# A fused two-block kernel: late modulation chunks inside the heads, routing on the unnormalised sum, the norm's gain applied to the gathered features

## The reference

```python
# first block
mix = hybrid_mixer(x, ...)                       # ends in merged @ w_out
h = layer_norm(ALPHA * x + mix, ln1_g, ln1_b)
logits = h @ router_w + router_b                 # 32 experts, the top 4 of each token
gates = softmax(top_4(logits))
ffn = sum over the chosen experts of gate * (act(h @ w_up[e] + b_up[e]) @ w_down[e] + b_down[e])
h = layer_norm(ALPHA * h + ffn, ln2_g, ln2_b)
# second block
mod = silu(c) @ w_ada + b_ada                    # sh1, sc1, g1, sh2, sc2, g2
h1 = ada_norm(x, norm1_g, sh1, sc1)
mixed = concat(neighbourhood(4 heads), latent(8 heads), conv)
mixed = rms_norm over groups of 64 (mixed) * out_norm_g
x = x + g1 * (mixed @ w_out_2)
x = x + g2 * ((silu(gt) * up) @ w_down_2)        # gt, up from ada_norm(x, norm2_g, sh2, sc2) @ w_gu
```

## Time and profile before

| | |
|---|---|
| runs | 1519.65, 1520.72, 1525.38 us |
| the profiled execution | 1522.91 us, span 1521.2 us from the first to the last instruction |
| TensorE matmul busy | 1421.0 us (93%) |
| VectorE, ScalarE, GpSimd busy | 585.2, 446.5, 39.4 us (38, 29, 3%) |
| read from memory | 514.75 MB, 339 GB/s over the span |
| mean granted clock of TensorE | 0.997 of full |

### The profile page before, as it was taken

How to read it: one execution, slowest core, us unless ns; L and a number is a source line. 1 busy time by engine, 2 the same in 40 slices (tenths; PEclk the granted TensorE clock), 3 DMA queues, 4 the chain that set the end, 5 groups by cost and what they waited for, 6 DMA issues and landing times. The chain is left out here.

```text
span 1521.2 us, 19879 instructions
## 1 busy us (share of the span) xinstructions
PE 1421.0 (93%) x8029; PEld 843.9 (55%) x8029; DVE 585.2 (38%) x979; ACT 446.5 (29%) x589; POOL 39.4 (3%) x81
## 2 busy tenths in 40 slices
PE   9999999999999999988988988989889999899998
PEld 9987897344434433333323433423334788788887
DVE  4984556210210221120210210210212685777765
ACT  5654533121112112112111111111102546454343
POOL 2000030000000000000000000000000022000000
PEclk9999999999999999999999999999999999999999
DMA  8597899999999999999999999999999451646552
GB/s 285 181 291 251 283 321 378 417 428 428 428 429 428 428 430 430 428 429 428 430 429 430 428 429 429 430 429 428 430 428 342 137 184 56 205 155 194 194 189 88
DMA packets 126952, 516.60 MB, mean 340 GB/s; under 512 B 6895, under 2 KB 95312, under 8 KB 102288
## 3 DMA queue, kind: packets, MB, share of 16 engines
q1 hardware_dynamic: 126032, 513.72, 84.8%
q10 hardware_dynamic: 864, 2.10, 0.5%
HBM read 514.75 MB, written 1.05 MB: 339 GB/s over the span
## 5 line engine op out<-in xcount | busy, mean ns | idle before, releaser
L1336 PE MATMUL ps<-ring,xg 128*64 128x512 f32 x1456 | 324.8, 595 | 25.1 <-DMA ring<-in_expert_w_up 22.1
L1485 DVE TENSOR_TENSOR glu<-ps,bupT 128x512 f32<-128x512 f32 x32 | 22.1, 692 | 718.8 <-PE ps L1345 718.8
L1336 PEld LDWEIGHTS ps<-ring,xg 128*64 128x64 f32 x1456 | 102.4, 137 | 241.5 <-issue 191.4
L88 ACT ACTIVATE hrow<-ps 128x1024 f32<-128x1024 f32 x32 | 32.8, 1024 | 472.3 <-PE ps L1336 472.3
L1361 PE MATMUL ps<-ring,act 128*64 128x512 f32 x608 | 136.2, 595 | 0.0
L2238 PE MATMUL ps<-h_halves,w_hi 128*128 128x512 f32 x352 | 122.1, 392 | 0.1
L2349 DVE TENSOR_TENSOR w_lo<-ring,w_hi 128x2048 fp32r<-128x2048 f32 x36 | 82.5, 2291 | 53.9 <-ACT w_hi L88 53.9
L1336 PE MATMUL ps<-more,xg 128*64 128x512 f32 x416 | 93.0, 595 | 8.7 <-DMA more<-in_expert_w_up 7.5
L2243 PE MATMUL ps<-h_halves,w_lo 128*128 128x256 f32 x348 | 97.5, 280 | 0.0
L88 ACT ACTIVATE w_hi<-ring 128x2048 fp32r<-128x2048 f32 (+1 forms) x38 | 70.9, 1866 | 71.9 <-PE ps L2243 31.1
L88 ACT ACTIVATE y<-ps 64x512 f32<-64x512 f32 x64 | 37.9, 592 | 181.8 <-PE ps L1361 181.5
(11 more groups left out here) (424 smaller groups left out, 2250.5 us busy)
## 6 DMA issues: line engine op xcount, KB each, us to landing
ring<-in_expert_w_up SPq DMA_DIRECT2D x91, 2048.0 KB, 36.1
ring<-in_expert_w_down SPq DMA_DIRECT2D x38, 2048.0 KB, 38.9
more<-in_expert_w_up SPq DMA_DIRECT2D x26, 2048.0 KB, 35.4
more<-in_expert_w_down SPq DMA_DIRECT2D x16, 2048.0 KB, 38.7
ring<-in_w_in SPq DMA_DIRECT2D x28, 1024.0 KB, 7.9
ring<-in_w_ada SPq DMA_DIRECT2D x24, 1024.0 KB, 5.4
x_xT_xn<-in_expert_w_up SPq DMA_DIRECT2D x11, 2048.0 KB, 36.7
ring<-in_w_gu SPq DMA_DIRECT2D x22, 1024.0 KB, 5.1
```

Source lines behind the costliest of these rows:

```text
L88: return nc.scalar.activation(out, x, ACT.Copy)
L1336: last = nc.tensor.matmul(up[a2 * CAP:(a2 + 1) * CAP, u, :], k.xg[:, q, h * CAP:(h + 1) * CAP], w[:, c:c + 512], start=(q == 0), stop=(q = ...
L1485: link(nc.vector.tensor_tensor(k.glu[:, :, :, :], g, b[:, 0].to_broadcast(wide), ALU.add))
```

## The change

Six edits, in the order of the program. (1) Eight rows of the first norm's gain and offset are loaded with the other parameter rows and turned by two more transposes into 16 more columns (`k.norm`). (2) In `branches` the residual sum is no longer normalised before it is turned and routed: GpSimd multiplies the router's weights by the gain (`k.rw_by`) and sums them over features, one product with ones adds these sums over partitions, and VectorE recovers the logits as the raw product times `rstd` plus an offset. The turns go between the pieces of `w_out` for tile 1, three of the four logit pieces and the last turn behind it. The rows of `k.h` become (x - mean) * rstd on ScalarE, off VectorE. (3) The softmax of the gates goes behind the selection on VectorE, their transposes into `experts`, and the second gate row behind the counting products. (4) The gathered tokens get gain and offset per feature, by eight ScalarE instructions of 128 columns in place of two copies of 512; `up_weights` waits for each of the eight. The residual `k.acc` takes four VectorE instructions in place of two. (5) `late_ada`: two of the four late chunks of `w_ada` are multiplied inside the heads, one in place of a filler product before the last head's turn, one behind the last head; the other two stay at the start of `output`. Two more `w_out_2` chunks may so be loaded during the heads. The `mix_sums` of the first eight heads move from head 10 to head 9. (6) In `output` ScalarE splits the second `w_out_2` chunk behind the eight `h_halves` instead of ahead of them.

```diff
-N_LATE_ADA = 4
+LATE_ADA = (22, 23, 20, 21)
+N_LATE_ADA = len(LATE_ADA)
...
-                        nc.tensor.transpose(k.ps[:, 7, 0:NROWS], k.rows, k.ident[0:NROWS, 0:NROWS])\
-                            .then_inc(rows_turned, 1)
+                        nc.tensor.transpose(k.ps[:, 7, 0:NROWS], k.rows, k.ident[0:NROWS, 0:NROWS])
+                        for j in range(2):
+                            last = nc.tensor.transpose(k.ps[:, 7, NROWS + 8 * j:NROWS + 8 * j + 8],
+                                                       k.norm_rows[:, j:2 * P:2], k.ident[0:8, 0:8])
+                        last.then_inc(rows_turned, 1)
...
+def late_ada(nc, k, pe, n):
+
+    w = last_arrived(k, pe, L_ADA + n)
+    for q in range(KD):
+        at = 32 * (q % 4)
+        last = nc.tensor.matmul(k.ps[at:at + 32, 7 - n // 2, (n % 2) * CH:(n % 2 + 1) * CH],
+                                k.cact[:, q:q + 1].to_broadcast([P, 32]), w[:, q, :],
+                                start=(n % 2 == 0 and q < 4), stop=(n % 2 == 1 and q >= 4), skip_group_check=True)
+    last.then_inc(k.last_used, 1)
+
...
+            def logits(t, half):
+                pe.wait_ge(hT_ready, max(3, order.index((t, half)) + 1))
+                for q in range(4 * half, 4 * half + 4):
+                    last = nc.tensor.matmul(k.ps[:, 4 + t, 0:E], hT[:, q, t * P:(t + 1) * P], k.rw_by[:, 1, q, :],
+                                            start=(q == 0), stop=(q == KD - 1))
                 return last
...
-            for t in range(TT):
-                for n in range(S_OUT + 4, S_OUT + 8):
-                    last = out_half(n, (t,))
-                last.then_inc(out_done, 1)
+            pe.wait_ge(rw_ready, 1)
+            nc.tensor.matmul(k.ps[:, 7, 0:2 * E].rearrange("p (g e) -> p g e", g=2), k.ones[:, :], k.rw_sum[:, :, 0, :],
+                             start=True, stop=True).then_inc(rw_summed, 1)
+            for n in range(S_OUT + 4, S_OUT + 8):
+                last = out_half(n, (0,))
+            last.then_inc(out_done, 1)
+            out_half(S_OUT + 4, (1,))
             turn(0, 0)
+            turn(1, 0)
+            out_half(S_OUT + 5, (1,))
             turn(0, 1)
-            pe.wait_ge(k.bcast_in, 16 * len(k.broadcasts))
+            out_half(S_OUT + 6, (1,))
+            out_half(S_OUT + 7, (1,)).then_inc(out_done, 1)
+            logits(1, 0)
+            turn(1, 1)
+            logits(0, 0)
+            logits(0, 1).then_inc(log_done, 1)
+            logits(1, 1).then_inc(log_done, 1)
             pe.wait_ge(gd, 1)
-            logits(0, range(4)).then_inc(log_done, 1)
             gate_row(0)
-            turn(1, 0)
-            logits(1, (0,))
-            turn(1, 1)
-            logits(1, (1, 2, 3)).then_inc(log_done, 1)
-            gate_row(1).then_inc(gb_done, 1)
...
+            gate_row(1).then_inc(gb_done, 1)
+            pe.wait_ge(z_done, TT)
             pe.wait_ge(k.hot_ready, 1)
             gather(nc, k, 5, range(4)).then_inc(k.g_done, 1)
...
             for t in range(TT):
+                if t == 0:
+                    evacuate(0, 0)
+                    evacuate(1, 0)
+                evacuate(t, 1)
                 act.wait_ge(var, t + 1)
                 nc.scalar.activation(k.root[:, t:t + 1], k.mv[:, t, 1:2], ACT.Sqrt, bias=k.eps[:, 0:1]).then_inc(root, 1)
-                evacuate(t, 0)
-                evacuate(t, 1)
+                act.wait_ge(z_scale, t + 1)
+                nc.scalar.activation(k.h[:, t, :], k.h[:, t, :], ACT.Identity, bias=k.small[:, 6 + t:7 + t],
+                                     scale=k.rstd[:, t:t + 1]).then_inc(z_done, 1)
             for t in range(TT):
                 act.wait_ge(negmax, t + 1)
...
+            pool.wait_ge(k.bcast_in, 16 * len(k.broadcasts))
+            for n in range(2):
+                by, w = (v.rearrange("p (b j) e -> p b j e", j=2) for v in (k.rw_by[:, n], k.rw[:, :, :]))
+                ins = nc.gpsimd.tensor_tensor(by, w, bc(k.norm[:, 1 - n], 3, E), ALU.mult)
+            link(ins)
+            link(nc.gpsimd.tensor_tensor(k.rw_sum, k.rw_by[:, :, 0:4], k.rw_by[:, :, 4:8], ALU.add))
+            link(nc.gpsimd.tensor_tensor(k.rw_sum[:, :, 0:2], k.rw_sum[:, :, 0:2], k.rw_sum[:, :, 2:4], ALU.add))
+            nc.gpsimd.tensor_tensor(k.rw_sum[:, :, 0, :], k.rw_sum[:, :, 0, :], k.rw_sum[:, :, 1, :], ALU.add)\
+                .then_inc(rw_ready, 1)
...
+                nc.vector.tensor_scalar(k.small[:, 6 + t:7 + t], k.mv[:, t, 0:1], k.rstd[:, t:t + 1], -1.0, ALU.mult, ALU.mult)\
+                    .then_inc(z_scale, 1)
+                dve.wait_ge(z_scale, t + 1)
+                link(nc.vector.scalar_tensor_tensor(out=k.offset[:, t, :], in0=k.col_sum, scalar=k.small[:, 6 + t:7 + t],
...
-                    if h == 0 and q % 4 == 0:
-                        pe.wait_ge(xg_ready, n * 2 + q // 4 + 1)
+                    if h == 0:
+                        pe.wait_ge(xg_ready, n * KD + q + 1)
...
-                    act_copy(nc, k.xg[:, 4 * half:4 * half + 4, :].rearrange("p k n -> p (k n)"), src[:, half, :])\
-                        .then_inc(xg_ready, 1)
+                    for j in range(4):
+                        q = 4 * half + j
+                        g, b = (k.norm[:, x, q // 2, q % 2:q % 2 + 1] for x in range(2))
+                        nc.scalar.activation(k.xg[:, q, :], src[:, half, j * P:(j + 1) * P], ACT.Identity, bias=b, scale=g)\
+                            .then_inc(xg_ready, 1)
 
...
-                nc.vector.tensor_scalar(k.acc[:, t, :], k.h[:, t, :], ALPHA, None, ALU.mult).then_inc(acc_done, 1)
+                start(nc.vector.scalar_tensor_tensor(out=k.acc[:, t, :], in0=k.h[:, t, :], scalar=ALPHA, in1=k.g1,
+                                                     op0=ALU.mult, op1=ALU.mult))
+                nc.vector.scalar_tensor_tensor(out=k.acc[:, t, :], in0=k.b1, scalar=ALPHA, in1=k.acc[:, t, :],
+                                               op0=ALU.mult, op1=ALU.add).then_inc(acc_done, 1)
...
-                    fill(nc, k, 7, k.gB[:, 0, 0:512], 1)
+                    pe.wait_ge(cv_out, 1)
+                    late_ada(nc, k, pe, 0)
...
             values(heads - 1)
+            late_ada(nc, k, pe, 1)
...
+                if i == 9:
+                    dve.wait_ge(o_out, 8)
+                    mix_sums(nc, k, link, 0, 8)
                 if i == 10:
-                    dve.wait_ge(o_out, 8)
                     dve.wait_ge(cv_out, 1)
                     mix_sums(nc, k, link, 12, 16)
-                    mix_sums(nc, k, link, 0, 8)
...
+            for n in (2, 3):
+                late_ada(nc, k, pe, n)
...
             high_w(L_OUT)
-            high_w(L_OUT + 1)
             for i, m in enumerate(BLOCKS):
                 act.wait_ge(mt, m // 2 + 1)
                 if i >= 4:
                     act.wait_ge(h_low, 0 + i - 3)
                 nc.scalar.activation(k.hhi[:, m, :], k.flat[:, m * T:(m + 1) * T], ACT.Copy,
                                      scale=k.cols[:, ROWS["onorm"] + m:ROWS["onorm"] + m + 1]).then_inc(h_high, 1)
+            high_w(L_OUT + 1)
```

More of the change, by code:

```diff
@@ L190, in last_chunks @@
     w = a["w_ada_2"][0].rearrange("(k p) n -> p k n", p=P)
-    for c in range(2 * N_ADA, 2 * N_ADA + N_LATE_ADA):
+    for c in LATE_ADA:
         out.append((w[:, :, c * CH:(c + 1) * CH], 8, CH))
@@ L1027, in _ @@
                 .then_inc(pos_done, 1)
-            pe.wait_ge(gate_ready, 1)
-            for t in range(TT):
-                last = nc.tensor.transpose(k.ps[0:E, 6, t * P:(t + 1) * P], k.gate[:, t, :], k.ident[:, :])
-            last.then_inc(gT_done, 1)
+            gate_row(1).then_inc(gb_done, 1)
+            pe.wait_ge(z_done, TT)
             pe.wait_ge(k.hot_ready, 1)
@@ L1172, in _ @@
                 normed(t)
-            for half in range(2):
-                dve.wait_ge(hT_done, half + 3)
-                nc.vector.tensor_copy(hT[:, 4 * half + 2:4 * half + 4, P:T],
-                                      k.ps[:, bank[1][half] + 4, 0:2 * P].rearrange("p (k n) -> p k n", k=2))\
-                    .then_inc(hT_last, 1)
             top(0)
@@ L1323, in _ @@
             gather(nc, k, 5, range(4, KD)).then_inc(g_done, 1)
+            for t in range(TT):
+                last = nc.tensor.transpose(k.ps[0:E, 3, t * P:(t + 1) * P], k.gate[:, t, :], k.ident[:, :])
+            last.then_inc(k.gT_done, 1)
             extra = extra_rounds(pe)
@@ L2157, in turned @@
                             ins.then_inc(done, 1)
-            for c in range(N_LATE_ADA):
-                w = last_arrived(k, pe, L_ADA + c)
-                for q in range(KD):
-                    at = 32 * (q % 4)
-                    last = nc.tensor.matmul(k.ps[at:at + 32, 6 + c // 2, (c % 2) * CH:(c % 2 + 1) * CH],
-                                            k.cact[:, q:q + 1].to_broadcast([P, 32]), w[:, q, :],
-                                            start=(c % 2 == 0 and q < 4), stop=(c % 2 == 1 and q >= 4),
```

(4 more changed lines are left out.)

109 lines of the change are left out of this document (56 added, 53 removed).

## The result

The changed kernel takes 1530.95 us (median of ten runs, 1528.55 to 1534.92) against 1523.24 us (ten runs) before: 1.0052 times the time, 95% interval 1.0041 to 1.0062. It is 7.7 us slower, where 1.4 us less was forecast (1519.3 us, on the median of three runs, 1520.72). The profiled execution is its slowest (1534.92, span 1533.1), so the two traces stand 11.9 us apart and not 7.7.

| | before | after | the stretch that ends here is longer by |
|---|---|---|---|
| first product of the first expert | 261.08 | 267.19 | 6.1 from the start |
| first product of the second block | 1176.68 | 1186.50 | 3.7 in the loop over the experts |
| first product of the output stage | 1295.17 | 1308.36 | 3.4 in the heads |
| end | 1521.2 | 1533.1 | -1.3 in the output stage |

A forecast was written before the change was run, and what follows sets the result against it. The prediction held the expert loop bound by reading weights from memory, leaving gains at its start and the heads/output border. Terms -0.6 + 1.7 - 2.5 = -1.4 us on 1520.7 gave 1519.3 us, range 1515.2 to 1522.8.

The forecast's parts named there:

- Edits costed at nothing: Routing and expert loop: added instructions, waits and loads were held to be covered by other work, at no cost.
- The stream from memory and not TensorE sets the pace: Expert loop: reading weights paces it, so the gain-and-offset instructions should not lengthen it; the argument against Rival 3.
- The prediction's own sign: Whole kernel: a time beyond 7.6 us from 1520.7 either way would mean the expert loop itself changed.
- Rival 3: Expert loop: gain-and-offset instructions come onto the path of every pair, 27 us more, 1546 us; chance 0.03.
- Term 1: Routing: logits and selection come earlier, so the first expert and its weight stream start earlier; -0.6 us.
- Rival 2: Routing: ScalarE's table load makes the first root late, up to 1.3 us onto the path, 1520.6 us; chance 0.13.
- Term 2: Heads' end: the moved sums of squares delay the last head's turn and a `w_ada` chunk follows; +1.7 us.
- rival 1: Heads' end: about 2.7 us of TensorE idleness halves the clock, costing 1.7 us more, 1521.0 us; chance 0.25.
- Term 3: Output's start: `h_halves` start earlier and the second `w_out_2` chunk's products begin near 13.2 instead of 15.7; -2.5 us.
- Sum: Whole kernel: the three terms add to -1.4 us against the median of 1520.7, giving 1519.3 us; chance 0.48.

The follow-up runs named there:

- e13: e10 with the norm's 16 columns kept in unused columns of `k.small`, so `x_hi` stands where the kernel before has it; 1519.51 us, ratio 0.9977.
- e12: Kernel before with 64 empty bytes ahead of `x_hi` and `x_lo` alone, all other tiles in place; 1526.18 us, ratio 1.0025.
- e11: Changed kernel with `k.cols` another 16 columns wider, so later tiles stand 128 and not 64 bytes further on; 1530.77 us, ratio 1.0046.
- e7: Changed kernel with `acc_done` awaited before `used`, the sums back at head 10, and later tiles shifted by 128 bytes instead of 64; 1523.27 us, ratio 0.9997.
- e8: Kernel before with only ScalarE's split of the second `w_out_2` chunk moved behind the eight `h_halves`; 1521.40 us, ratio 0.9986.
- e10: e7 with the first gate row ahead of tile 0's logits and a 512-column filler product where it stood; 1521.13 us, ratio 0.9987.
- e9: Kernel before with two late `w_ada` chunks inside the heads, sums not moved, and the second `w_out_2` split behind `h_halves`; 1521.14 us, ratio 0.9985.

## Why the prediction was wrong

**Edits costed at nothing.** This is the step that failed. The prediction went through the waits on TensorE's and SyncE's queues, and did not see the wait added on ScalarE ahead of `hrow`, which makes the loop 3.7 us longer. "The stream from memory and not TensorE sets the pace" was true only up to the slack: TensorE waited 22.1 + 7.5 + 3.8 = 33.4 us for weights in the loop before, 10.7 after. 19.0 us of loads and the half-speed stretches ate the difference. The prediction's own sign for this came: a time over 7.6 us from 1520.7 would mean that the loop itself changed, and it is 10.2 above. Rival 3 did not come; with the same eight gain-and-offset instructions e13's loop takes 915.2 us. Nor did the prediction ask what else the widened `k.cols` moves. In the kernel before, e12 prices that at 3.6 us, 2.1 of them at like clock. In the two traces at the top, which share a fall of 6.8 us near 113 us, `w_out` ends 5.1 us later where 2.1 were predicted. In the changed kernel's medians the price is not shown: shifting by 128 bytes instead gained 0.2 us (e11) and 0.7 (e7).

**Term 1** was right as a chain and lacked the clock. `w_out` ends 2.0 us later (243.6 in e7, 241.6 in e8, both without falls; predicted 1.8 and two turns), and from there it takes 12.8 us at full clock (e11), 3.2 less than before. That is -1.2 us (-0.6 predicted), and +3.2 with the fall. Only the part behind `w_out` is firm: e10, with e7's instructions up to there and no fall either, ends `w_out` at 245.6. e13, at the pace of the kernel before and with the same early fall, starts its first expert 2.7 us before it. Rival 2 did not come: the root was there before `w_out` ended.

**Term 2** was mis-sized, as rival 1 said: +3.4 us in this trace (+1.7 predicted) and up to +5.2. The idle time was 2.44 us where 2.7 was forecast, and the fall followed in four traces of four; 0.25 was too low a chance. But the price of the sums was a choice: behind the last head's maxima they cost nothing, late chunks included (118.5 us in e13).

**Term 3** was right: -2.44 us at the second chunk (13.28 for 15.72), with a wait of 1.17 us where 1.3 was predicted. Only 1.3 of it is left at the end, since later products of this stage run at other distances from execution to execution: a pair of 512 and 256 columns stands 0.347 us from the next before and in e9, which keeps 2.4, but 0.355 in the later part of the changed kernel's trace, and 0.356 in e13, whose stage takes 226.0 us as before.

**Sum.** With the four costs mended, which took back the move of the sums and added a filler, e13 takes 1519.51 us, 3.6 below before. The forecast missed the costs. That e13 comes so near to its 1519.3 is luck: the forecast stood on a median 2.4 us lower than the one beside e13, and held 1.7 us for the sums.

**What stays open.** Why 64 bytes cost most, and 32 and 128 little. Why the unshifted program runs its split products at 0.113 us in some executions and at 0.118 in others. How the 7.7 us divide: by medians, each against the kernel before in its own series, the sums give 4.4 back, the wait order 2.6 on top of them, the bytes 0.7, the filler with the earlier gate row 1.4 and e13's return to the old place 2.2, each measured behind the others and with falls that come and go.

## What to carry to other kernels

When a change adds a wait, look on that engine for a table load ahead of the waiting instruction, and let the wait that is met last come last. That a loop is bound by memory gives TensorE a slack with a size: add up what it waits for memory there, and compare that with what the change adds. Before explaining a stretch where nothing was changed, look whether its operands moved, and try a version with empty bytes.

## What the runs showed of the hardware

- 64 empty bytes ahead of the moving operand (e12): products of 128x256 at 0.120 us instead of 0.113 to 0.118, at granted clock 1.00, and 3.6 us on the median, 2.1 at like clock.
- A table load of 1283 ns runs ahead of its instruction's own wait, but behind a wait that is an instruction of its own: 0.3 against 188.4 us of idle time before fourteen loads.
- The clock fell to 0.50 behind products of 32 columns, with TensorE busy 3.45 of the 3.60 us before the fall. In the loop it fell in 8 pairs of 15 with a wait of 2.48 us, and in none with a wait of 1.2; at the border of heads and output it fell at 1.98 or 1.99 us of idle time in six traces of seven, and at 0.98 or 0.99 in none of seven.
